# Means of a two-block transformer kernel's norms: from one fp32 product with ones to two fp32r products, of a rounded part and the rest

## What is computed

```python
def rms_norm(x, g):
    xf = x.astype(jnp.float32)
    y = xf * lax.rsqrt(jnp.mean(xf * xf, axis=-1, keepdims=True) + EPS)
    return (y * g.astype(jnp.float32)).astype(x.dtype)
...
        o_a = o_a * lax.rsqrt(jnp.mean(o_a * o_a, axis=-1, keepdims=True) + EPS)
...
    q = rms_norm(heads(q_sb), q_norm_g)
    k = rms_norm(heads(k_sb), k_norm_g)
...
    hn = rms_norm(h, norm2_g)
    ffn = (jax.nn.silu(hn @ w_gate) * (hn @ w_up)) @ w_down
```

## Time and profile before

| | |
|---|---|
| median of 3 runs | 1386.57 us (1385.87 to 1387.39) |
| the profiled execution | 1385.86 us; its span 1384.6 us |
| TensorE busy | 1376.7 us (99%) |
| VectorE busy | 624.3 us (45%) |
| ScalarE busy | 834.1 us (60%) |
| GpSimd busy | 211.6 us (15%) |
| mean granted TensorE clock | 1.000 |

### The profile page before, as it was taken

One profiled execution on the slowest core, in us unless ns is written; L12 is line 12 of the kernel. 1 busy time (PEld: TensorE's weight loads), 2 busy tenths in 40 slices (PEclk: granted clock), 3 DMA queues, 4 the chain that ended last, 5 costly groups with the idle time before them and its releaser, 6 DMA issues.

```text
span 1384.6 us, 17401 instructions
## 1 busy us (share of the span) xinstructions
PE 1376.7 (99%) x6778; PEld 1116.8 (81%) x6778; DVE 624.3 (45%) x1217; ACT 834.1 (60%) x1241; POOL 211.6 (15%) x259
## 2 busy tenths in 40 slices
PE   9999999999999999999999999999999999999999
PEld 6977966788888888887877788888888888888887
DVE  6055366521211212356488888975434312331241
ACT  6565576654544545666488677775666645663661
POOL 0211100111111111111211111211111111111111
DMA  7975644788888988877665665677879888889875
GB/s 253 243 166 124 150 114 96 170 201 196 189 194 197 194 188 197 185 171 177 152 143 121 135 148 123 138 151 174 197 178 213 192 191 195 191 195 196 190 169 120
DMA packets 68327, 239.55 MB, mean 173 GB/s; under 512 B 7602, under 2 KB 7915, under 8 KB 68116
## 3 DMA queue, kind: packets, MB, share of 16 engines
q0 software_dynamic: 36144, 130.32, 52.0%
q1 hardware_dynamic: 31236, 106.24, 24.0%
q10 hardware_dynamic: 864, 1.87, 0.4%
HBM read 236.28 MB, written 2.12 MB: 172 GB/s over the span
## 4 chain that ended last, share of the span: by engine, by line
PE 92%; ACT 3%; DVE 3%; DMA 1%; issue 1%; SPq 0%; POOL 0%; ACTq 0%; DVEq 0%
PE bank L501 28%; PE bank L508 28%; PE bank L505 28%; PE bank L616 1%; PE bank L635 1%; PE bank L659 1%; PE bank L649 1%; PE bank L684 1%; DVE eb L1453 1%; DMA RAW<-in_w_in 1%; DMA WH<-in_w_in 1%; PE bank L667 0%; ACT WL L814 0%; DVE eb L1449 0%; ACT WH L806 0%
## 5 line engine op out<-in xcount | busy, mean ns | idle before, releaser
L501 PE MATMUL bank<-NH,WH 128*128 128x512 f32 x1152 | 465.4, 405 | 0.2 <-ACT NH L970 0.2
L505 PE MATMUL bank<-NL,WH 128*128 128x512 f32 x1152 | 448.4, 390 | 0.5 <-DVE NL L1197 0.5
L508 PE MATMUL bank<-NH,WL 128*128 128x512 f32 x1152 | 448.1, 390 | 0.2 <-DVE WL L1192 0.2
L806 ACT ACTIVATE WH<-RAW 128x1024 fp32r<-128x1024 f32 (+3 forms) x196 | 201.8, 1031 | 197.7 <-PE bank L508 190.8
L501 PEld LDWEIGHTS bank<-NH,WH 128*128 128x128 f32 x1152 | 216.5, 188 | 62.9 <-issue 21.1
L505 PEld LDWEIGHTS bank<-NL,WH 128*128 128x128 f32 x1152 | 216.8, 188 | 46.3 <-issue 3.8
L508 PEld LDWEIGHTS bank<-NH,WL 128*128 128x128 f32 x1152 | 216.4, 188 | 46.6 <-DVE WL L1192 0.6
L814 ACT ACTIVATE WL<-WH 128x1024 fp32r<-128x1024 f32 (+2 forms) x219 | 229.2, 1047 | 18.4 <-DMA WH<-in_w_in 13.2
L505 PE MATMUL bank<-AL,WH 128*128 128x512 f32 x432 | 168.2, 389 | 0.0
L501 PE MATMUL bank<-AH,WH 128*128 128x512 f32 x432 | 168.1, 389 | 0.0
L508 PE MATMUL bank<-AH,WL 128*128 128x512 f32 x432 | 168.1, 389 | 0.0
(11 more groups left out here) (326 smaller groups left out, 1648.1 us busy)
## 6 DMA issues: line engine op xcount, KB each, us to landing
RAW<-in_w_ff SPq DMA_DIRECT2D x64, 512.0 KB, 6.1
WL<-in_w_ff POOLq DMA_DIRECT2D x64, 512.0 KB, 8.7
WL<-in_w_in POOLq DMA_DIRECT2D x62, 512.0 KB, 7.0
RAW<-in_w_gu SPq DMA_DIRECT2D x44, 512.0 KB, 7.0
WL<-in_w_gu POOLq DMA_DIRECT2D x44, 512.0 KB, 8.6
RAW<-in_w_in SPq DMA_DIRECT2D x32, 512.0 KB, 7.3
WH<-in_w_in POOLq DMA_DIRECT2D x32, 512.0 KB, 6.8
RAW<-in_w_down SPq DMA_DIRECT2D x20, 512.0 KB, 4.5
```

What stands on the lines that cost most here:

```text
L501: e.matmul(o, a[0], a[1], start=(k == 0), stop=False)
L505: e.matmul(o, b[0], b[1], start=False, stop=False)
L508: mm = e.matmul(o, c[0], c[1], start=False, stop=(k == t.kt - 1))
L806: e.activation(WH[p % HL][:, 0:n], RAW[raw_slot[p]][:, 0:n], ACT.Copy).then_inc(*act.sig("high", p))
```

## The change

Sixteen of the means (the two FFN norms, the two of "second", four GLA heads, eight tiles of q and k) are computed from two parts. ScalarE writes the rounded sum (`mean_high`, type fp32r), VectorE the rest, sum minus rounded sum (`mean_low`, fp32r), and TensorE issues two fp32r products of the same constants into the same bank (`mean_of`). The constants are rounded in place once (`ones`); 1/1024, 1/64 and 0 stay what they are. The mean of the first norm ("attn") remains one fp32 product and now waits for `ones`. The planned times of these means and of their roots are later. q and k get four sets of buffers: the two new ones lie in rows 0 to 2 of `hB` and `vH`, whose own first writers (`hg_f` and `natural`) get a wait for the last k tile. The line `qk_start` loses its distance of 12.4. The rounded views (`sq_r`, `gt_r`, `ft_r`, `qk_high`, `qk_low`) lie on the places of the fp32 buffers.

```diff
+sq_r, gt_r, ft_r = rounded("sq", 2), rounded("gT", 2), rounded("ft1", 6)
+qk_sq = wT + [hB[:, 0, :], vH[:, 0, :]]
+qk_y, qk_a = zb[0:2] + [hB[:, 1, :], vH[:, 1, :]], eb2 + [hB[:, 2, :], vH[:, 2, :]]
+qk_high = rounded("zb", 2) + [rounded_row("hB", 1), rounded_row("vH", 1)]
+qk_low = rounded("eb", 2) + [rounded_row("hB", 2), rounded_row("vH", 2)]
...
-mean_time = {"attn": 24.0, "mlp": plan.start(("f1", 0)) + 7.3, "ffn": plan.start(("gu", 0)) + 6}
-T_DS = plan.start("qS") + 8
-ready = {"n_attn": 28.0, "n_mlp": mean_time["mlp"] + 3.3, "n_ffn": mean_time["ffn"] + 3.3, "n_second": T_DS + 15.0}
+mean_time = {"attn": 24.0, "mlp": plan.start(("f1", 0)) + 9, "ffn": plan.start(("gu", 0)) + 8}
+T_DS = plan.start("qS") + 9
+ready = {"n_attn": 28.0, "n_mlp": mean_time["mlp"] + 3.3, "n_ffn": mean_time["ffn"] + 3.3, "n_second": T_DS + 14.5}
...
-    qk_start.append(max(due(t), qk_start[-2] + 12.4 if len(qk_start) > 1 else 0, qk_start[-1] + 2 if qk_start else 0))
+    qk_start.append(max(due(t), qk_start[-1] + 2 if qk_start else 0))
...
-        pe.wait_ge(("const",), ("square_sum", ph, 7), *free)
-        e.matmul(bank, ones1k, acc, start=True, stop=True).then_inc(*pe.sig("mean", ph))
+        if ph == "attn":
+            pe.wait_ge(("ones_rounded",), ("square_sum", ph, 7), *free)
+            e.matmul(bank, ones1k, acc, start=True, stop=True).then_inc(*pe.sig("mean", ph))
+        else:
+            pe.wait_ge(("mean_low", ph), *free)
+            mean_of(bank, ones_r[0], *sq_r).then_inc(*pe.sig("mean", ph))
+    def mean_of(bank, ones, high, rest):
+        e.matmul(bank, ones, high, start=True, stop=False)
+        return e.matmul(bank, ones, rest, start=False, stop=True)
...
-        pe.wait_ge(("square_sum", "second", 7), *free)
-        e.matmul(bank, ones1k, acc, start=True, stop=True).then_inc(*pe.sig("mean", "second"))
-        pe.wait_ge(("square_sum_2", 7), *free2)
-        e.matmul(bank2, ones1k, acc2, start=True, stop=True).then_inc(*pe.sig("mean", "scaled"))
+        pe.wait_ge(("mean_low", "second"), *free)
+        mean_of(bank, ones_r[0], *sq_r).then_inc(*pe.sig("mean", "second"))
+        pe.wait_ge(("mean_low", "scaled"), *free2)
+        mean_of(bank2, ones_r[0], ft_r[4], ft_r[5]).then_inc(*pe.sig("mean", "scaled"))
...
-            yield head_time(c, hh, 2)
+            yield head_time(c, hh, 3.6)
...
-            pe.wait_ge(("gla_square", h), *free)
-            e.matmul(bank, ones1k, gb_[1], start=True, stop=True).then_inc(*pe.sig("gla_mean", h))
+            pe.wait_ge(("mean_low", ("gla", h)), *free)
+            mean_of(bank, ones_r[0], *gt_r).then_inc(*pe.sig("gla_mean", h))
...
-            yield qk_time(t, 7.5)
+            yield qk_time(t, 9.5)
...
-            pe.wait_ge(("qk_square", st, t.i), *free)
-            e.matmul(bank, ones64, wT[t.i % 2], start=True, stop=True).then_inc(*pe.sig("qk_mean", st, t.i))
+            pe.wait_ge(("mean_low", (st, t.i)), *free)
+            mean_of(bank, ones_r[2], qk_high[t.i], qk_low[t.i]).then_inc(*pe.sig("qk_mean", st, t.i))
...
+def mean_high(key, x, to, *waits):
+    act.wait_ge(*waits)
+    act.e.activation(to, x, ACT.Copy).then_inc(*act.sig("mean_high", key))
+def mean_low(key, x, high, to):
+    dve.wait_ge(("mean_high", key))
+    dve.e.tensor_tensor(to, x, high.bitcast(F32), ALU.subtract).then_inc(*dve.sig("mean_low", key))
...
+    def ones():
+        yield 16.0
+        act.wait_ge(("const",))
+        e.activation(ones_all, cf[:, P:4 * P], ACT.Copy).then_inc(*act.sig("ones_rounded"))
...
+        if ph != "attn":
+            yield time - 1.8
+            mean_high(ph, acc, sq_r[0], ("square_sum", ph, 7))
...
+        yield T_DS - 4.0
+        mean_high("second", acc, sq_r[0], ("square_sum", "second", 7), ("square_sum_2", 6))
+        mean_high("scaled", acc2, ft_r[4], ("square_sum_2", 7))
...
+            if st == "vH":
+                act.wait_ge(("qk", "kS", 3))
...
-            yield head_time(c, hh, 2) + 0.2
-            root_act(("gla", h), bank_of("gla_mean", h), d0, ("gla_mean", h), ("gla_x", c, 256, 1), unit=8.0)
+            mean_high(("gla", h), ee, gt_r[0], ("gla_square", h), ("gla_x", c, 256, 1))
+            yield head_time(c, hh, 3.6) + 0.2
+            root_act(("gla", h), bank_of("gla_mean", h), d0, ("gla_mean", h), unit=8.0)
...
-            u, o = t.i % 2, (qS if st == "qS" else kS)[:, t.i, :]
-            back = [("qk", st, t.i - 2)] if t.i >= 2 else [("qk", "qS", t.i + 2)] if st == "kS" else second_end
+            u, o = t.i, (qS if st == "qS" else kS)[:, t.i, :]
+            back = [("qk", "qS", t.i)] if st == "kS" else second_end
...
-            e.activation(wT[u], o, ACT.Square).then_inc(*act.sig("qk_square", st, t.i))
-            yield qk_time(t, 7.7)
-            root_act(("qk", st, t.i), bank_of("qk_mean", st, t.i), zb[u], ("qk_mean", st, t.i))
+            e.activation(qk_sq[u], o, ACT.Square).then_inc(*act.sig("qk_square", st, t.i))
+            yield qk_time(t, 1.5)
+            mean_high((st, t.i), qk_sq[u], qk_high[u], ("qk_square", st, t.i))
+            yield qk_time(t, 9.7)
+            root_act(("qk", st, t.i), bank_of("qk_mean", st, t.i), qk_y[u], ("qk_mean", st, t.i))
...
-            act.wait_ge(("hf_f", t.i))
+            act.wait_ge(("hf_f", t.i), ("qk", "kS", 3))
...
-    streams = [prologue(), splits(), negated(), root("attn", mean_time["attn"]), columns("attn", 30.0)]
+    streams = [prologue(), ones(), splits(), negated(), root("attn", mean_time["attn"]), columns("attn", 30.0)]
...
+        if ph != "attn":
+            yield time - 0.9
+            mean_low(ph, acc, *sq_r)
...
+        yield T_DS - 2.5
+        mean_low("second", acc, *sq_r)
+        mean_low("scaled", acc2, ft_r[4], ft_r[5])
...
-            yield head_time(c, hh, 3)
-            root_square(("gla", h), d0, d1, ("gla_x", c, 128, 1))
-            yield head_time(c, hh, 4)
+            yield head_time(c, hh, 2.2)
+            mean_low(("gla", h), gb_[1], *gt_r)
+            yield head_time(c, hh, 4.4)
+            root_square(("gla", h), d0, d1)
+            yield head_time(c, hh, 5.1)
...
-            yield head_time(c, hh, 5)
+            yield head_time(c, hh, 5.8)
...
-            yield head_time(c, hh, 6)
+            yield head_time(c, hh, 6.5)
...
-            u, o = t.i % 2, dst[:, t.i, :]
-            y, a, key, bank = zb[u], eb2[u], ("qk", st, t.i), ("qk_mean", st, t.i)
+            u, o = t.i, dst[:, t.i, :]
+            y, a, key, bank = qk_y[u], qk_a[u], ("qk", st, t.i), ("qk_mean", st, t.i)
...
-            yield qk_time(t, 8.7)
+            yield qk_time(t, 3.5)
+            mean_low((st, t.i), qk_sq[u], qk_high[u], qk_low[u])
+            yield qk_time(t, 10.7)
...
-            yield qk_time(t, 9.7)
+            yield qk_time(t, 11.7)
...
-            yield qk_time(t, 10.7)
+            yield qk_time(t, 12.7)
```

More of the change, by code:

```diff
@@ L223, in build_program @@
         top = [(nc.sbuf_base + 63) // 64 * 64]
+        places = {}
         def sb(name, cols, dt=F32, parts=P):
@@ L228, in sb, with rounded @@
             top[0] = place + (size + 63) // 64 * 64
+            places[name] = place
             assert top[0] <= nc.sbuf_usable_end, (name, top[0], nc.sbuf_usable_end)
             return nc.alloc_sbuf_tensor_at(name, [parts, cols], dt, offset=place)[:, :]
+        def rounded(name, n):
+            return [nc.alloc_sbuf_tensor_at(f"{name}{i}_r", [P, S], F32R, offset=places[f"{name}{i}"])[:, :] for i in range(n)]
         def rows_of(name, k, dt=F32):
@@ L250, in build_program @@
         cf = sb("cf", 4 * P + S)
-        ident, ones1k, turn, ones64 = (cf[:, i * P:(i + 1) * P] for i in range(4))
+        ident = cf[:, 0:P]
         gmask = cf[:, 4 * P:4 * P + S]
+        ones_all = nc.alloc_sbuf_tensor_at("ones_r", [P, 3 * P], F32R, offset=places["cf"] + 4 * P)[:, :]
+        ones_r = [ones_all[:, i * P:(i + 1) * P] for i in range(3)]
+        ones1k, turn, ones64 = (a.bitcast(F32) for a in ones_r)
         rs, acc = sb("rs", S), sb("acc", S)
@@ L312, in build_program, with rounded_row @@
         AH2, AL2, ft2 = rows_of("AH2", 8, F32R), rows_of("AL2", 8, F32R), two("ft2", 6)
+        def rounded_row(name, row):
+            return nc.alloc_sbuf_tensor_at(f"{name}_r{row}", [P, S], F32R, offset=places[name] + row * S * 4)[:, :]
+        sq_r, gt_r, ft_r = rounded("sq", 2), rounded("gT", 2), rounded("ft1", 6)
[3 more added lines that the diff above has]
+        qk_low = rounded("eb", 2) + [rounded_row("hB", 2), rounded_row("vH", 2)]
         ps = [ctx.enter_context(nc.psum_tensor(f"bank{i}", [P, S], F32))[:, :] for i in range(8)]
```

## The result

The changed kernel takes **1391.14 us** (median of 7 runs, 1390.33 to 1392.3), the kernel before 1386.62 us in the same session: ratio 1.0035, 95% interval [1.0026, 1.0045], slower by 4.5 us. The forecast was 1391.6 us, +5.0.

A forecast was written before the change was run, and what follows sets the result against it. TensorE, busy 1376.7 of 1384.6 us, was taken as the bound. Terms -6.6 + 0.1 + 1.2 + 10.3 = +5.0 us against the profiled 1385.86 gave 1390.9, median 1391.6 us; range 1384.5 to 1395.5.

The forecast's parts named there:

- One mean, -0.41: TensorE, sixteen means: one fp32 product of 0.87 us becomes two fp32r products at 0.23, saving 6.6 us in all.
- attn, mlp, ffn: 0 or 0.1: First norm and two FFN norms: later inputs cost nothing at attn and ffn, 0.1 us at mlp.
- GLA: 0: Four GLA heads: means stand 6 or 12 products later, so later inputs cost 0, with 0.4 us spare behind the last.
- "second": 1.05 + 0.15: Norm "second": TensorE waits 1.05 us, then 0.15, for its two rests; cost 1.2 us, first Ln at 614.47.
- q's first root 635.3, k's first tile out 645.65, its rest 649.6: Head norms, VectorE and ScalarE: times in us leading to k's first rest, which TensorE wants at 645.3.
- Rounds of 8.6, 7.7 and 7.8: Head norms: us per round of VectorE and ScalarE from one k rest to the next, against TensorE's 5.9, 6.0 and 6.2.
- Waits of 4.3, 2.7, 1.7 and 1.6: Head norms: us TensorE waits at k's four means for their rests, 10.3 us in all.
- the ring: Head norms: VectorE and ScalarE wait for each other, each k tile and rest standing behind roots; 8.6, 7.7, 7.8 us a round.
- The engines keep up: Head norms: ScalarE and VectorE keep pace and TensorE does not wait; -5.3 us, 1381.3 us; chance 12%.
- Rival 2: Head norms: only k's first wait is real, rounds stay within 6 us; cost 4.3, time 1385.6 us; chance 8%.
- Rival 3: vS: weight pieces queued on ScalarE behind k's squares come late and run short once; 1394 to 1395 us; chance 7%.
- Rival 4: All sixteen means: the two products take as long as the one, the 6.6 us gain is gone; 1395.3 us; chance 2%.

The follow-up runs named there:

- experiment 5: Changed kernel with 18 dummy fp32r products ahead of k's first mean, overwritten by it: 1390.56 us.
- experiments 2 and 3: Changed kernel with the head norms of q and k put back: 1384.64 us; with the norm "second" put back as well: 1384.16 us.
- experiment 10: Changed kernel, "second" later, q's means and roots earlier, head-norm steps reordered (Ln and Exp before the next tile's square, rest inside the root): 1382.78 us.
- experiment 6: Changed kernel with k's four means 7 to 11 units later in TensorE's list alone: 1398.88 us.
- experiment 7: Changed kernel with the head norms' roots at least 5.2 units apart: 1388.3 us.
- experiment 9: Kernel of experiment 8 with q's means and roots about 3 units earlier, roots at least 4.6 units apart: 1388.22 us.
- the simple half: Changed kernel with the head norms of q and k as before the change, all other means but attn's split: 1384.64 us.
- the half with the ring: Changed kernel with only the head norms of q and k split, the other eight means fp32 at their old times: 1393.18 us.
- experiment 4: Changed kernel with the norm "second" 2 units later in every list: 1389.39 us.
- experiment 8: Kernel of experiment 7 with the norm "second" 2 units later in every list: 1385.97 us.

## Why the prediction was right

- *One mean, -0.41.* Held. TensorE's products and the new means start 0.23 apart. The Trainium skill (TensorE: Matmul & The Clock Gate, Back-to-back issue gap) has 131 ns for a product of 512 columns; no trace here comes near it. Even the 18 dummy products of experiment 5, with one and the same weight tile, start 0.23 apart (their record of 4.24 us, less 0.39 for the last of them, is 17 such distances).
- *attn, mlp, ffn: 0 or 0.1.* Held: no wait at any of them.
- *GLA: 0.* Held for the rests, and not for the cost. The prediction looked behind the last head only; the bank that the next head's first product takes comes free later, and that costs 0.5 us (experiments 2 and 3).
- *"second": 1.05 + 0.15.* The trace has 0.88 and a gap that is not listed; first Ln at 614.58 against 614.47. Moving it later gave 1.6 with the head norms changed (+4.5 to +2.9), some of it by another order on VectorE, and 0.8 without (-2.2 to -3.0), where 1.2 was forecast; neither difference is clear of its intervals.
- *q's first root 635.3, k's first tile out 645.65, its rest 649.6.* Measured 635.42, 645.65 and 649.53. That the very times agree has luck in it. They were counted on the old kernel's time line, and the prediction said "less 2", the gain up to there. In this execution the gain was 1.5 (GLA 1.1, mlp 0.4) and the late start 1.5, so that TensorE came to "second" 0.03 us from the old time. The distances are what was forecast: 14.1 us from q's first root to k's first rest. The working through two in-order lists was worth its length: everything in it came from durations of the kernel before. The Trainium skill (PSUM — Partial Sum Buffer, Engine vs sequencer instructions) says that the queues of ScalarE and VectorE are strictly first in, first out; the rest that stood for 1.9 us behind a root's first step agrees.
- *Rounds of 8.6, 7.7 and 7.8.* The rests are ready at 649.53, 658.07, 665.68 and 673.41: 8.5, 7.6 and 7.7.
- *Waits of 4.3, 2.7, 1.7 and 1.6.* Measured 4.16, 0, 1.03 and 1.3. The step that failed in its form is the second: TensorE's distance was to be 5.9 us at full clock, and it was 8.95, because the clock fell behind the first wait. The prediction has no term for the clock. The end didn't move, since the ring set it. From behind "second" to the end of k's means TensorE falls 6.8 us behind; -0.41 x 8 + 10.3 = 7.0 was forecast.
- *The total.* 4.5 by the medians, 5.0 forecast. Product by product, measured for forecast: GLA -1.1 for -1.6, mlp -0.4 for -0.3, "second" +0.5 for +0.4, the head norms +6.8 for +7.0, ffn -0.4 for -0.4. Then -0.4 at 772 us in the stick-breaking stage, which nobody forecast and whose cause is open; it happens to make up for GLA. With the late start (+1.5) and 0.4 us behind the last product, which every later profile has too, these are the 6.0 between the two profiled executions.
- *The rivals.* "The engines keep up" was wrong for this order and right for another (experiment 10). Its place in the forecast was judged by the order, not by the busy shares of 46% and 61%, and that was the right measure. Rival 2 is near the list of waits, where the second is missing, but not near the time, since the slow products stand in its place. Rival 3 shows only in experiment 6. Rival 4 is excluded by the 0.46 us of a new mean.

What I had wrong was the cure, three times: later means (6), spread roots (7) and earlier roots (9) each move one wait in a ring of three engines. Only counting who waits for whom once around showed which two steps to exchange.

## What to carry to other kernels

Where two in-order engines pass work back and forth, write one round out as a list of both and look for an idle stretch on each in it: if both idle, it is the order and not the load that is too slow, however small the busy shares are. A wait of TensorE can have a second price behind it, products at the lower clock. Experiment 5 shows that it cost nothing where the ring set the end; that it counts where TensorE does is my inference, no run isolates it. Split a change of many sites by site before judging it: here the simple half gave 2.2 us, and the half with the ring took 6.3. Where two instructions are put ahead of a mean, look also at what its root frees for the next stage, as at GLA.

## What was not expected of the hardware

The clock fell at some waits and not at others of the same length. In the changed kernel it was at 1.2 GHz for 13 products, and it fell before TensorE began again: of its wait (645.43 to 649.59) the part up to 649.0 has full clock, the rest half. The other waits of single means come in pairs that went both ways:

- 3.6 us (experiment 4): it fell. 3.5 us (experiment 7): it stayed up.
- 2.44 us (experiment 5): it fell, for 8 products. 2.44 us (experiment 9): it stayed up.
- 1.84 us (experiment 8): it fell, for 8 products, 1.5 us after the wait. 1.85 us (experiment 10): it stayed up.

A window of experiments 7, 9, 8 and 10 each, the same columns. The first two take in the whole wait, the third the end of it, the last what follows it:

```profile
650.00:660.00 10.00, 6.43 (x36) 1.00 0.48 84
656.00:668.00 12.00, 9.56 (x73) 1.00 0.45 98
644.00:650.00 6.00, 5.18 (x16) 0.72 0.81 185
652.00:656.00 4.00, 4.00 (x20) 1.00 0.46 89
```

What decides between them no run here tells; the length of the wait alone doesn't. The cost of a wait of 1.8 to 2.4 us was so between nothing and 1.6 us more (8 products at 0.20).
